# Order of banks, weight preparation and x transposes in the second block's up product of a fused transformer kernel

## The reference

```
hid = rmsnorm(x, g_pre_ffn) @ w_up              # 512 x 1024 @ 1024 x 5632
hid = depthwise convolution of hid over 3 tokens + conv_b
a, b = split(hid, 2)                            # 2816 channels each
x = x + rmsnorm((gelu(a) * b) @ w_down, g_post_ffn)
```

## Time and profile before

| quantity | value |
|---|---|
| median of 3 runs | 2285.42 us |
| the profiled execution | 2285.36 us |
| its span, first to last instruction | 2283.5 us |
| mean granted TensorE clock | 0.999 |
| TensorE busy | 2253.8 us (99%) |
| VectorE busy | 1426.5 us (62%) |
| ScalarE busy | 968.7 us (42%) |
| second block's up stage | about 1904 us to 2154 us of the span |
| down stage | about 2158 us to 2278 us |

### The profile page before, as it was taken

How to read it: one execution, slowest core, us unless ns; L and a number is a source line. 1 busy time by engine, 2 the same in 40 slices (tenths; PEclk the granted TensorE clock), 3 DMA queues, 4 the chain that set the end, 5 groups by cost and what they waited for, 6 DMA issues and landing times.

```text
span 2283.5 us, 30232 instructions
## 1 busy us (share of the span) xinstructions
PE 2253.8 (99%) x11144; PEld 1883.1 (82%) x11144; DVE 1426.5 (62%) x1867; ACT 968.7 (42%) x1375; POOL 80.8 (4%) x115
## 2 busy tenths in 40 slices
PE   7999999999999999999999999999999999999999
PEld 5788888888888788888888888888888889788887
DVE  7899864444335898964444434664676568888723
ACT  4577644343223587644433223432443434323322
POOL 1000010000001000010000001000000000000000
PEclk9999999999999999999999999999999999999999
DMA  4211223222223211222222233222122231222222
GB/s 173 72 56 56 75 92 107 96 92 86 89 93 114 92 56 54 77 92 93 92 104 93 76 101 133 92 91 102 73 74 81 86 128 39 92 100 102 101 92 74
DMA packets 32073, 205.06 MB, mean 90 GB/s; under 512 B 3552, under 2 KB 3936, under 8 KB 11360
## 3 DMA queue, kind: packets, MB, share of 16 engines
q1 hardware_dynamic: 31968, 203.66, 25.4%
HBM read 201.55 MB, written 2.10 MB: 89 GB/s over the span
## 4 chain that ended last, share of the span: by engine, by line
PE 90%; DVE 5%; issue 2%; ACT 2%; DMA 0%; DVEq 0%; SPq 0%; ACTq 0%
PE mm L1644 26%; PE mm L1646 26%; PE mm L1645 26%; PE misc L1667 2%; PE sp L1645 1%; PE sp L1646 1%; PE sp L1644 1%; PE ob L1644 1%; DVE conv_y L1045 1%; PE sp L1735 1%; PE ob L1645 1%; PE ob L1646 1%; DVE w_lo L970 1%; PE sp L1751 1%; PE ob L1744 1%
## 5 line engine op out<-in xcount | busy, mean ns | idle before, releaser
L1644 PE MATMUL mm<-in_hi,w_hi 128*128 128x512 f32 (+1 forms) x1920 | 757.5, 395 | 18.9 <-DVE w_lo L970 10.9
L1646 PE MATMUL mm<-in_hi,w_lo 128*128 128x512 f32 (+1 forms) x1920 | 745.6, 388 | 0.0
L1645 PE MATMUL mm<-in_lo,w_hi 128*128 128x512 f32 (+1 forms) x1920 | 744.9, 388 | 0.0
L469 ACT ACTIVATE w_hi<-w_raw 128x2048 fp32r<-128x2048 f32 (+2 forms) x193 | 346.7, 1796 | 671.4 <-PE mm L1646 666.8
L970 DVE TENSOR_TENSOR w_lo<-w_raw,w_hi 128x2048 fp32r<-128x2048 f32 (+2 forms) x196 | 439.5, 2243 | 227.4 <-ACT w_hi L469 227.0
L1644 PEld LDWEIGHTS mm<-in_hi,w_hi 128*128 128x128 f32 x1920 | 361.3, 188 | 98.9 <-issue 19.5
L1645 PEld LDWEIGHTS mm<-in_lo,w_hi 128*128 128x128 f32 x1920 | 361.5, 188 | 76.0 <-issue 4.1
L1646 PEld LDWEIGHTS mm<-in_hi,w_lo 128*128 128x128 f32 x1920 | 361.0, 188 | 75.1
L1045 DVE SCALAR_TENSOR_TENSOR conv_y<-conv_in,parl,conv_y 128x512 f32<-128x512 f32 x240 | 169.9, 745 | 1.7
L981 DVE TENSOR_TENSOR tB<-mm,rstd 128x512 f32<-128x512 f32 x56 | 38.7, 691 | 173.7 <-PE mm L1646 173.7
L1644 PE MATMUL mm<-act_hi,w_hi 128*128 128x512 f32 x352 | 136.9, 389 | 0.0
(11 more groups left out here) (426 smaller groups left out, 3333.5 us busy)
## 6 DMA issues: line engine op xcount, KB each, us to landing
w_raw<-in_w_dram SPq DMA_DIRECT2D x160, 1024.0 KB, 4.8
w_raw<-in_w_dram SPq DMA_DIRECT2D x32, 704.0 KB, 4.0
w_raw<-in_w_dram SPq DMA_DIRECT2D x6, 512.0 KB, 5.6
out_dram<-z_rows SPq DMA_DIRECT2D x8, 256.0 KB, 2.0
rope<-in_rope_dram SPq DMA_DIRECT2D x3, 512.0 KB, 3.4
x<-in_x_dram SPq DMA_DIRECT2D x1, 1024.0 KB, 10.8
dist<-in_distances_dram SPq DMA_DIRECT2D x1, 896.0 KB, 5.2
x<-in_x_dram SPq DMA_DIRECT2D x1, 768.0 KB, 8.0
```

The costliest lines, as they stand in the source:

```text
L469: e.activation(whi[:, slot, 0:cols], raw[:, slot, 0:cols], ACT.Copy).then_inc(s_whi, whi_out.up())
L1644: MM(out, ah, bh, start=first, stop=False, **kw)
L1645: MM(out, ah, bl, start=False, stop=False, **kw)
L1646: return MM(out, al, bh, start=False, stop=last, **kw)
```

## The change

Three things are changed in this stage. The up product uses four banks in turn: even pairs `mm0`, `mm1`, odd pairs the two of `spf[0]`. The weights of chunk m + 2 are made ahead of pair m's takes instead of after its product, on VectorE and on ScalarE. The row blocks of x are assigned to banks in another order (`spf[1]`; `ob` and `misc`; `mm`; `spf[0]`), and the transposes and copies of the last row block move into the first chunk of the down product.

```diff
+        up_banks = [(mm[0][:], mm[1][:]), (spf[0][:, 0:T], spf[0][:, T:2 * T])]
+        rows = [(spf[1][:, 0:T], spf[1][:, T:2 * T]), (ob[:], mi[:]), *up_banks]
# ScalarE
-            def gated_conv(m, c, early=False):
-                if not early:
-                    tiles.skip(2)
+            def gated_conv(m):
                 taken.skip(2)
                 e.wait_ge(s_val, val.next())
                 e.activation(tC[:], tC[:], ACT.Gelu_apprx_tanh).then_inc(s_fn, fn.up())
-                if not early:
-                    prep(c)
                 e.wait_ge(s_val, val.next())
                 hi(tile(acth, m), tD[:])
+            def next_weights(c):
+                tiles.skip(2)
+                prep(c)
+            gated_conv(0)
+            next_weights(1)
+            gated_conv(1)
+            with L.loop(1, S_UP // 2 - 1) as i:
+                for c in range(2):
+                    next_weights(c)
+                    gated_conv(i * 2 + c)
+            next_weights(0)
+            gated_conv(FT - 2)
+            for b in range(TB - 1):
+                x_rows(b)
+            next_weights(1)
+            x_rows(TB - 1)
+            gated_conv(FT - 1)
# VectorE
+            def gated_product(m):
                 e.wait_ge(s_do, own.now())
                 e.wait_ge(s_fn, fn.next())
                 TT(tD[:], tC[:], tD[:], ALU.mult).then_inc(s_val, val.up())
-                if not early:
-                    prep(c, cols)
                 lo(tile(actl, m), tD[:], tile(acth, m))
+            gated_conv(0, B_CV, up_banks[0])
+            prep(1)
+            gated_conv(1, B_CV + 8, up_banks[1])
+            with L.loop(1, S_UP // 2 - 1) as i:
+                b0 = e.snap(i * 16)
+                for c in range(2):
+                    prep(c)
+                    gated_conv(i * 2 + c, b0 + (B_CV + 8 * c), up_banks[c])
+            prep(0)
+            gated_conv(FT - 2, B_CV + 8 * (FT - 2), up_banks[0])
+            take_up(tA, up_banks[1][0])
+            take_up(tB, up_banks[1][1])
+            prep(1)
+            three_taps(B_CV + 8 * (FT - 1), tA, tC).then_inc(s_val, val.up())
+            three_taps(B_CV + 8 * (FT - 1) + 4, tB, tD).then_inc(s_do, own.up())
+            gated_product(FT - 1)
# TensorE
+            with L.loop(1, S_UP // 2):
+                for c, pair_of in enumerate(up_banks):
+                    e.wait_ge(s_w, w_in.next())
+                    for d, bank in enumerate(pair_of):
+                        e.wait_ge(s_mmf, taken.next())
+                        half_product(bank, whi[:, c, :], wlo[:, c, :], CH // 2 * d,
+                                     slice(0, T)).then_inc(s_mm, tiles.up())
+            for b in range(TB - 1):
+                turn_x(b)
             last = S_DOWN - 1
             for c in range(last - 1):
                 e.wait_ge(s_w, w_in.next())
                 for b in range(TB):
+                    if c == 0 and b == TB - 2:
+                        turn_x(TB - 1)
                     for d in range(2):
                         ins = rows_product(c, b, d)
```

More of the change, by code:

```diff
@@ L288, in program @@
         gout = sq[:, :, :].rearrange("p a t -> p (a t)")
-        rows = [(spf[0][:, 0:T], spf[0][:, T:2 * T]), (spf[1][:, 0:T], spf[1][:, T:2 * T]), (ob[:], mi[:]),
-                (mm[0][:], mm[1][:])]
+        up_banks = [(mm[0][:], mm[1][:]), (spf[0][:, 0:T], spf[0][:, T:2 * T])]
+        rows = [(spf[1][:, 0:T], spf[1][:, T:2 * T]), (ob[:], mi[:]), *up_banks]
         halves = (slice(0, TH), slice(TH, T))
@@ L910, in gated_conv, with x_rows @@
                 e.activation(tC[:], tC[:], ACT.Gelu_apprx_tanh).then_inc(s_fn, fn.up())
-                if not early:
-                    prep(c)
                 e.wait_ge(s_val, val.next())
                 hi(tile(acth, m), tD[:])
[L916 to L923, removed]
+            def next_weights(c):
+                tiles.skip(2)
+                prep(c)
+            def x_rows(b):
+                for d, bank in enumerate(rows[b]):
                     e.wait_ge(s_xt, 2 * b + d + 1)
                     e.activation(xr[:, b, d * T:d * T + T], bank, ACT.Copy).then_inc(s_xe, 1)
-            gated_conv(FT - 1, 1)
+            gated_conv(0)
[12 more added lines that the diff above has]
+            gated_conv(FT - 1)
             e.preload_act_table_set(LN_EXP)
@@ L1580, in _, with take_up, three_taps @@
             e.wait_ge(s_fn, fn.next())
[L1582 to L1593, removed]
+            def take_up(src, bank):
+                e.wait_ge(s_mm, tiles.next())
+                TT(src[:, 1:T + 1], bank, rstd[:], ALU.mult).then_inc(s_mmf, taken.up())
+            def three_taps(b, src, dst):
+                e.wait_ge(s_mmf, taken.now())
+                step(TS(dst[:], src[:, 0:T], col(pars, b), col(pars, b + 3), ALU.mult, ALU.add))
+                step(STT(dst[:], src[:, 1:T + 1], col(pars, b + 1), dst[:], ALU.mult, ALU.add))
+                return STT(dst[:], src[:, 2:T + 2], col(pars, b + 2), dst[:], ALU.mult, ALU.add)
+            def gated_product(m):
                 e.wait_ge(s_do, own.now())
@@ L1596, in gated_conv @@
                 TT(tD[:], tC[:], tD[:], ALU.mult).then_inc(s_val, val.up())
-                if not early:
-                    prep(c, cols)
                 lo(tile(actl, m), tD[:], tile(acth, m))
-            gated_conv(0, B_CV, 0, early=True)
-            gated_conv(1, B_CV + 8, 1, banks=(spf[0][:, 0:T], spf[0][:, T:2 * T]))
+            def gated_conv(m, b0, banks):
+                take_up(tA, banks[0])
+                three_taps(b0, tA, tC).then_inc(s_val, val.up())
+                take_up(tB, banks[1])
+                three_taps(b0 + 4, tB, tD).then_inc(s_do, own.up())
+                gated_product(m)
+            gated_conv(0, B_CV, up_banks[0])
+            prep(1)
+            gated_conv(1, B_CV + 8, up_banks[1])
             with L.loop(1, S_UP // 2 - 1) as i:
                 b0 = e.snap(i * 16)
[L1605 to L1608, removed]
+                for c in range(2):
[9 more added lines that the diff above has]
+            gated_product(FT - 1)
             for c in range(2, S_DOWN):
@@ L1983, in _, with turn_x @@
                     small(ones, ssum[:], rot)
[L1984 to L1995, removed]
+            with L.loop(1, S_UP // 2):
[5 more added lines that the diff above has]
+                                     slice(0, T)).then_inc(s_mm, tiles.up())
+            def turn_x(b):
+                left, right = rows[b]
+                if b == 1:
                     e.wait_ge(s_msf, misc_taken.next())
-                if b == 3:
+                if b > 1:
                     e.wait_ge(s_mmf, taken.next(2))
```

## The result

The changed kernel takes 2305.16 us, the median of 4 runs (2304.29 to 2305.72), against 2285.67 us for the kernel before in the same comparison. The ratio is 1.0085, with a 95% interval of 1.0073 to 1.0098: slower by 19.5 us. The forecast was 2306.6. The profiled execution took 2305.05 us, its span is 2303.2.

A forecast was written before the change was run, and what follows sets the result against it. TensorE, busy 99% of the span, was taken to bound the kernel. A down product 19.0 us later, 0.8 for the fourth row block and 1.4 for the clock give 21.2 over 2285.36: 2306.6 us, 8-in-10 range 2299 to 2313.

The forecast's parts named there:

- What goes: TensorE before chunk 3: the 3.70 us stop and 1.49 us of slow matmuls go, together 5.2 us.
- T(1): Start of pair 1's take of tile A on VectorE, forecast at 1939.96.
- The chain: Up loop, VectorE and ScalarE: take through product, high copy, w_hi, w_lo to next take, 12.14 us against TensorE's 10.88.
- T(19): Start of pair 19's take of tile A, forecast at 2157.4 after 17 passes of 12.14 us.
- T(m) to P(m): Part of each loop pass, from start of pair m's take of tile A to start of its product: 6.62 us.
- The end of the stage: Transposes and copies of x come late: down product starts 19.0 us later, at 2177.1, after stops of 2.1 and 3.2.
- Edits costed at nothing: Down product's weights, SyncE's loads and takes from other banks were each taken to add 0 us.
- A: Rival: no chain, TensorE never stops in the loop, needing a pass of at most 10.88 us; 2280.2 us, chance 0.06.
- B: Rival: clock falls in the loop's short stops and stays down for whole tiles; +18 us, about 2325, chance 0.03.
- C: Rival: loop as forecast, but the tail is hidden and no clock is lost; 2299.9 us, chance 0.09.
- D: Rival: pass longer by 0.3 us or more from exposed waits between engines; 2312 us and up, chance 0.09.
- E: Rival: gains and losses meet within 0.2%, 2280.9 to 2290.0 us, with a pass of about 10.7 to 11.2; chance 0.03.

The follow-up runs named there:

- Experiment 8: Changed kernel with only chunk 3's weights made ahead and the loop's weights in the earlier kernel's order; 2285.85 us, ratio 1.0.
- experiment 1: Changed kernel with ScalarE's copy to w_hi put ahead of the high copy again, all else as changed; 2281.39 us, ratio 0.998.
- experiment 5: Changed kernel with ScalarE's copy to w_hi done twice in a row for chunks 3 to 23; 2344.51 us, ratio 1.0258.
- experiment 6: Kernel before the change with the copy to w_hi done twice for chunks 3 to 23; 2286.76 us, ratio 1.0005.
- Experiment 4: Changed kernel with ScalarE copying the first two row blocks of x ahead of pair 20's high copy; 2300.32 us, ratio 1.0063.
- Experiment 3: Changed kernel's banks and order of x only, with the weights in the earlier kernel's order; 2283.98 us, ratio 0.9991.
- experiment 2: Changed kernel with weights one pair ahead but in the earlier kernel's order within a pair, on both engines; 2279.74 us, ratio 0.9974.
- experiment 7: Changed kernel with two banks instead of four for pairs from 2 on, weights still ahead; 2423.72 us, ratio 1.0604.

## Why the prediction was right

The forecast was 2306.6 us, the measured time is 2305.16. By its steps:

**What goes.** T(1) was forecast at 1939.96 and stands at 1939.93:

```profile
1939.93 0.69 DVE L1592 TENSOR_TENSOR tA<-sp,rstd 128x512 f32<-128x512 f32 x1
```

No stop follows it, and the stop of 3.70 us with its slow matmuls is gone. Experiment 8 adds what the prediction did not say: it goes only because later chunks' weights also come early.

**The chain.** This is the step that carries the result, and experiments 1, 5 and 6 show it. It was reckoned at 12.14 us. The first pass of the loop took 12.15 (1950.98 to 1963.13), the later ones 11.99 to 12.07; T(19) is 2155.62, so the 17 passes are 12.04 on average. The term mis-sized is T(m) to P(m): 6.62 came from the loop's first pass, whose idle gaps between taps are longer than later ones. In the changed kernel it is 6.62 in the first pass too, and then 6.49 and 6.56 in turn. The other four terms agree within 0.02 us. Over 17 passes this is 1.8 us, the whole error of the forecast at that point.

One reason given beside the chain does not hold. The prediction says that the four banks don't help because a second slot for `w_hi` and `w_lo` is not there. There are two slots, and no wait for one: in the loop `w_hi` starts right behind the high copy, and TensorE had left its slot 7 to 8 us before (chunk 4 ended at about 1964.3, and `w_hi` of chunk 6, which takes over its slot, starts at 1971.00). It is the order of the instructions alone that ties the weights to the pass.

**Where the stops begin.** Forecast: chunk 6 first, about 0.8 us, then about 1.26 us in each chunk. Measured: chunk 6 with 0.56 us, then 0.78 to 0.89. The passes are 12.04 - 10.88 = 1.16 us over TensorE's own. The stops are shorter than that by the way the profile counts: it takes a matmul as 0.39 us long, 0.16 more than the 0.23 from start to start, and the restart behind a stop takes 0.1.

**The end of the stage.** Two stops of 2.1 and 3.2 us were forecast and 1.82 and 3.03 found. The down product was forecast at 2177.1 and began at 2175.24, early by the 1.9 us that the passes were short. From T(20), 2167.62, it is 7.62 us, and 7.6 were reckoned. Experiment 4 confirms that the copies behind the high copy set this start. The fall of the clock was the least certain term, taken at 1.4 with bounds of 0 and 1.5; it cost 1.6. So the total, 1.4 us under the forecast, is 1.9 from the passes less 0.2 from the clock, and a rest within the scatter.

**Edits costed at nothing.** Experiment 3 bounds the four banks and the new order of x together at no cost.

**The rivals.** A, TensorE never stops in the loop, is false for the change but true of experiments 1 and 2. It had been put at 2280.2. Experiment 2, which has no stop at the end of the stage either, came to 2279.7, and experiment 1, with one of 1.70 us there, to 2281.4. What decides between A and the forecast is one ScalarE instruction on one side or the other of a wait. A's condition, a pass of at most 10.88 us, was too strict: experiment 1 meets A's outcome with 10.97. The break-even pass of 10.98 is too low, as 18 passes, not 17, lie ahead of T(20), where the tail begins: 12.14 - 19.8/18 = 11.04. Experiment 1 lies 0.07 under that in each pass and began the loop 2.7 us earlier, which together are the 4 us by which it beats the kernel before. B did not happen: behind the short stops of the loop the granted clock stayed at 1.00. This window of the changed kernel holds 15 of the 16 (length, TensorE busy, granted clock, DMA share, GB/s):

```profile
1956.00:2153.00 197.00, 184.63 (x796) 1.00 0.25 88
```

The Trainium skill ("TensorE: Matmul & The Clock Gate", section "A second HAM failure mode: psum-queue depth-cycling") reports of another kernel that small idles between groups of matmuls, with PSUM banks in turn, made the clock swing. This trace does not agree for stops of 0.56 to 0.89 us. For the long stops of experiment 7 the clock did fall. C and D did not happen: the tail was not hidden, and the pass was shorter than reckoned, not longer. E, gains and losses that meet, is out by the 19.5 us.

## What to carry to other kernels

When a step is moved ahead on two engines, write down for each engine what it now stands behind, and follow the crossings in a ring: work that used to lie between two waits of an in-order engine, and so cost nothing, can become a link of the chain on the other side of one wait. Compare the sum of the ring with the bound engine's time for the same pass; here 12.0 against 10.9 decided the matter, though neither engine of the ring was full: over the window above VectorE was busy for 74% and ScalarE for 26%. Over a stage of few passes a ring slightly longer than that pass can still hide behind a head start (experiment 1).

Prepare ahead by shifting the index (work for pair m + 1 in the old place) before changing the order within a pair: experiment 2 has all the gain of the early weights and none of the ring. And before a single stop is mended, ask which engine is behind there; mending its last cause alone moves the stop on (experiment 8).

## What the runs showed of the hardware

In these traces the length of a stop alone does not tell whether the clock falls behind it. In experiment 5 two stops of the same 2.77 us, two passes apart, were followed by slow and by fast matmuls (the distance from the first to the next start is 0.59 us at half clock, 0.34 at full):

```profile
2011.86 0.79 PE L1667 MATMUL mm<-in_hi,w_hi 128*128 128x512 f32 x1 [2.77 <-DVE tA L1595]
2012.45 0.63 PE L1668 MATMUL mm<-in_lo,w_hi 128*128 128x512 f32 x1
...
2039.82 0.50 PE L1667 MATMUL mm<-in_hi,w_hi 128*128 128x512 f32 x1 [2.77 <-DVE tA L1595]
2040.16 0.39 PE L1668 MATMUL mm<-in_lo,w_hi 128*128 128x512 f32 x1
```

The granted clock (third from the end) behind the first and behind the second:

```profile
2014.00:2018.00 4.00, 4.00 (x11) 0.50 0.35 145
...
2042.00:2046.00 4.00, 4.00 (x19) 1.00 0.35 147
```

Ahead of the first TensorE had run one chunk at full clock behind a stop of 1.29 us; ahead of the second it had run two chunks without a stop between them, the earlier one partly at half clock. The next stop, 2.84 us, was followed by full clock too, and the one after it, 2.75 us, by half.

Stops of 1.70 (experiment 1) and 2.48 us (experiment 3) left the clock up; those of 3.03 (the changed kernel, 0.9 us of work behind one of 1.82), 3.67 (experiment 8) and 4.93 (experiment 7) were followed by half clock. In experiment 5 the falls cost nothing: behind a chunk that had run slowly the next stop was 1.2 to 1.3 us instead of 2.8 (twice there was none), and from the second pass of the loop on the takes stayed 13.94 to 14.03 us apart, as the chain alone gives.
